# One 4 MB DMA for an expert's down weights, with gate and up columns read in runs of four

## The reference

```
z   = RMSNorm(x) @ W_in
a   = GatedDeltaNet(4 heads x 128)          chunks of 64
b   = DilatedSWA(8 heads x 64)              three (window, dilation) branches
h   = x + concat(a, b) @ W_out
out = h + MoE(RMSNorm(h))                   top 4 of 32 experts
```

```python
logits = hf @ w_router + b_router
top_v, top_e = lax.top_k(logits, 4);  gates = softmax(top_v)
# for every expert e and the tokens xblk that chose it:
gu   = xblk @ w_gu[e] + b_gu[e]                  # (tokens, 2048)
gate = minimum(gu[:, :1024], 7);  up = clip(gu[:, 1024:], -7, 7)
act  = (up + 1) * gate * sigmoid(1.702 * gate)
y    = act @ w_dn[e] + b_dn[e]                   # (tokens, 1024)
out += gate_weight * y
```

## Time and profile before

| | us |
|---|---|
| median of 3 runs | 1098.6 (1098.51 to 1100.0) |
| the profiled execution's own time | 1100.03 |
| its span | 1098.3 |
| PE busy | 1029.1 (94%) |
| DVE, ACT, POOL busy | 281.4, 162.4, 14.0 |
| bytes moved | 427.73 MB, 389 GB/s over the span |

### The profile page before, as it was taken

The page is one execution under the profiler, slowest core; times in us unless marked ns, Lnnn a source line. Parts: engine busy times, 40 slices in busy tenths (PEclk is TensorE's granted clock), DMA queues, the critical chain, the costliest instruction groups (busy, mean ns, idle before and its releaser), DMA issues.

```text
span 1098.3 us, 12632 instructions
## 1 busy us (share of the span) xinstructions
PE 1029.1 (94%) x4986; PEld 428.1 (39%) x4986; DVE 281.4 (26%) x667; ACT 162.4 (15%) x271; POOL 14.0 (1%) x34
## 2 busy tenths in 40 slices
PE   9999999999999999999999988888999898899987
PEld 7855566443434344443333222222333332233232
DVE  3754553522222232222211101111111111111111
ACT  4513355001000000001001000000000000000001
POOL 3001000000000000000000000000000000000000
PEclk9999998999999999999999989999999999999999
DMA  9577288799999999999999999999999999999996
GB/s 327 114 240 311 77 302 330 306 428 426 428 419 428 428 430 434 428 431 428 429 428 427 431 431 430 436 428 427 431 431 432 428 430 431 429 430 428 428 428 269
DMA packets 40186, 427.73 MB, mean 389 GB/s; under 512 B 8371, under 2 KB 10644, under 8 KB 20180
## 3 DMA queue, kind: packets, MB, share of 16 engines
q1 hardware_dynamic: 38884, 426.63, 93.3%
q10 hardware_dynamic: 1264, 0.56, 0.2%
HBM read 424.42 MB, written 2.75 MB: 389 GB/s over the span
## 4 chain that ended last, share of the span: by engine, by line
PE 52%; DMA 38%; DVE 6%; ACT 2%; issue 1%; SPq 0%; DVEq 0%; ACTq 0%
DMA store<-in_w_gate_up_dram 21%; PE bank L2036 18%; DMA store<-in_w_down_dram 16%; PE bank L2086 14%; PE bank L1590 3%; PE bank L1597 3%; PE bank L1953 2%; PE bank L1685 2%; PE bank L1817 2%; PE bank L2016 1%; DVE flow L1445 1%; PE bank L2055 1%; DVE flow L1438 1%; DVE flow L1443 1%; ACT flow L893 1%
## 5 line engine op out<-in xcount | busy, mean ns | idle before, releaser
L2036 PE MATMUL bank<-store,flow 128*64 128x512 f32 x2048 | 451.1, 596 | 14.1 <-DMA store<-in_w_gate_up_dram 13.2
L2036 PEld LDWEIGHTS bank<-store,flow 128*64 128x64 f32 x2048 | 144.2, 137 | 315.7 <-issue 288.8
L2086 PE MATMUL bank<-store,flow 128*64 128x512 f32 x992 | 227.6, 610 | 37.3 <-DMA store<-in_w_down_dram 25.0
L1438 DVE TENSOR_SCALAR flow<-bank 128x512 f32<-128x512 f32 x32 | 22.1, 691 | 605.5 <-PE bank L2036 605.5
L2086 PEld LDWEIGHTS bank<-store,flow 128*64 128x64 f32 x992 | 72.9, 140 | 171.0 <-issue 141.4
L893 ACT ACTIVATE flow<-flow 128x512 f32<-128x512 f32 x32 | 20.2, 630 | 448.4 <-DVE flow L1438 448.4
L1962 PE MATMUL bank<-qkT 64*128 64x512 f32 x248 | 61.9, 616 | 0.0
L1590 PE MATMUL bank<-store 128*128 128x512 f32 x128 | 57.2, 595 | 0.0
L909 ACT COPY qkT<-bank 128x512 f32<-128x512 f32 x31 | 18.1, 585 | 206.2 <-PE bank L2086 206.2
L903 ACT COPY flow<-flow 128x512 f32 x30 | 33.8, 1125 | 22.8 <-DVE flow L1419 13.3
L1962 PEld LDWEIGHTS bank<-qkT 64*128 64x128 f32 x248 | 21.3, 186 | 40.1 <-issue 40.1
(11 more groups left out here) (333 smaller groups left out, 598.1 us busy)
## 6 DMA issues: line engine op xcount, KB each, us to landing
store<-in_w_gate_up_dram SPq DMA_DIRECT2D x38, 4096.0 KB, 27.1
store<-in_w_down_dram SPq DMA_DIRECT2D x60, 2048.0 KB, 19.1
store<-in_w_gate_up_dram SPq DMA_DIRECT2D x51, 2048.0 KB, 15.2
store<-in_w_in_dram SPq DMA_DIRECT2D x6, 2048.0 KB, 15.9
store<-in_w_out_dram SPq DMA_DIRECT2D x1, 4096.0 KB, 12.9
store<-in_w_down_dram SPq DMA_DIRECT2D x3, 1024.0 KB, 30.7
store<-in_w_gate_up_dram SPq DMA_DIRECT2D x2, 1024.0 KB, 6.3
flow<-in_w_down_dram SPq DMA_DIRECT2D x1, 2048.0 KB, 11.8
```

Source lines behind the costliest of these rows:

```text
L1438: dve.tensor_scalar(gt, bank[4][:], LIMIT, None, ALU.min).then_inc(g_min, 1)
L2036: ins = mm(dst[SLOTS * hf:SLOTS * (hf + 1), :], rows[:, c:c + SLOTS], store[:, slot_at(j, odd) + c0:slot_at(j, odd) + c0 + 512], start=Fal ...
L2086: ins = mm(dst[SLOTS * hf:SLOTS * (hf + 1), :], turned[:, c:c + SLOTS], w[:, hf * 512:(hf + 1) * 512], start=f == 0, stop=f == KT - 1)
```

## The change

1. The down weights of a block are loaded in one DMA of 4 MB where `load_block` is called with `whole` (blocks 9 on), and for the first of the last three blocks with gate and up tiles apart (`whole_down=True`). Partition p holds rows 8p to 8p + 7 of the matrix, 32 KB in a run. The DMA waits until both down halves of the block before are used. TensorE's first down half then waits for the whole tile (`ld_tile[4]`), the second for nothing.
2. Half tiles that stay (early blocks, the last two) hold the rows 8p + 4h + c: 16 KB in a run, at a step of 32 KB in DRAM. The second half still waits for `ld_tile[5]`.
3. The activations have to come in that order. Half hf of the gate (and up) columns is now the columns 8r + 4hf + c, so the moving operand of L2036 reads four values and skips four.
4. The bias rows are put in the same order: the four bias DMAs bring 1024 (or 1020) columns each to `extra[:, 0:D]`, and one ACT copy takes four of every eight values into `bgu`. SP waits for this copy ahead of the load into `extra[:, 0:D]`, TensorE ahead of block 0.

```diff
+        bgu_rows = extra[:, 0:D]
...
-            half = tile - 4
-            src = w_down[0][e_ap, half * 4 * P:(half + 1) * 4 * P, :]
-            return src.rearrange("a (p c) n -> p (a c n)", p=P)
+            return w_down[0][e_ap, :, :].rearrange("a (p h c) n -> p h (a c n)", p=P, h=2)[:, tile - 4]
...
+        def expert_down(e_ap):
+            return w_down[0][e_ap, :, :].rearrange("a (p c) n -> p (a c n)", p=P)
+
+        def act_columns(ap):
+            return ap.rearrange("p (r h c) -> p h r c", h=2, c=4)
...
             for c in range(4):
-                sp.dma_start(bgu[N_EXP * c:N_EXP * (c + 1), :], b_gate_up[0][:, c * 512:(c + 1) * 512]
+                n = D - 4 * (c % 2)
+                sp.dma_start(bgu_rows[N_EXP * c:N_EXP * (c + 1), 0:n], b_gate_up[0][:, (c // 2 + 1) * D - n:(c // 2 + 1) * D]
                              ).then_inc(ld_moe, 16)
...
+            sp.wait_ge(bgu_ready, 1)
             sp.dma_start(extra[:, 0:D], expert_tile(slice(1, 2), 4)[:, 0:D]).then_inc(ld_extra, 16)
...
-            def load_down(m, e, off):
+            def load_down(m, e, off, whole):
+                if whole:
+                    sp.wait_ge(wdn_used, 2 * m + 2 * off)
+                    sp.dma_start(store[:, slot_at(8):slot_at(8) + 4 * SLOT], expert_down(bass.ds(e, 1))
+                                 ).then_inc(ld_tile[4], 16)
+                    return
                 for hf in range(2):
                     sp.wait_ge(wdn_used, 2 * m + (2 * off + hf - 1))
...
-            load_block(five_less, expert_of(five_less + 1), expert_of(three_less), 0, False, off=1, tiled=FINE_BLOCKS)
+            load_block(five_less, expert_of(five_less + 1), expert_of(three_less), 0, False, off=1, tiled=FINE_BLOCKS, whole_down=True)
...
+            act.wait_ge(ld_moe, 16 * 6)
+            Tally(act, bgu_ready).mark(act.copy(bgu.rearrange("p (r c) -> p r c", c=4),
+                                                bgu_rows.rearrange("p (r c) -> p r c", c=8)[:, :, 0:4]))
             h_sums(1)
...
                 if early and not b:
-                    pe.wait_ge(ld_moe, 16 * 6)
+                    pe.wait_ge(bgu_ready, 1)
...
-                order = [(bank[4], 0, 0), (bank[4], 1, 512), (bank[5], 0, 1024), (bank[5], 1, 1536)]
+                order = [(bank[4], 0, 0), (bank[4], 1, 0), (bank[5], 0, D), (bank[5], 1, D)]
...
-                                     store[:, slot_at(j, odd) + c0:slot_at(j, odd) + c0 + 512], start=False,
+                                     act_columns(store[:, slot_at(j, odd) + c0:slot_at(j, odd) + c0 + D])[:, hf], start=False,
...
-                elif not last:
-                    pe.wait_ge(ld_tile[4 + half], 16 * (b + 1) if early else 16 * b)
+                elif not last and half == 0:
+                    pe.wait_ge(ld_tile[4], 16 * (b + 1) if early else 16 * b)
+                elif not last and halves is not None:
+                    pe.wait_ge(ld_tile[5], 16 * halves)
```

More of the change, by code:

```diff
@@ L359, in hybrid_layer @@
         up_step, out_left, out_right, st_right = (sem(n) for n in ("up_step", "out_left", "out_right", "st_right"))
+        bgu_ready = sem("bgu_ready")
         seeded, cnt_read = sem("seeded"), sem("cnt_read")
@@ L546, in load_early, with load_block @@
                 sp.dma_start(tile_dst(4), expert_tile(slice(3, 4), 4)).then_inc(ld_tile[4], 16)
-            def load_block(m, e, e_next, down_at, whole, off=0, tiled=None):
+            def load_block(m, e, e_next, down_at, whole, off=0, tiled=None, whole_down=None):
                 odd = sp.value_load(parity[0:1, bass.ds(m + (off + 1), 1)], min_val=0, max_val=1)
@@ L554, in load_block @@
                     if half == down_at:
-                        load_down(m, e, off)
+                        load_down(m, e, off, whole if whole_down is None else whole_down)
                     if whole:
@@ L2065, in turns, with down @@
                 pe.wait_ge(SGT_ready, b + 1)
-            def down(b, half, last_at=None):
+            def down(b, half, last_at=None, halves=None):
                 last = last_at is not None
@@ L2088, in down, with rest @@
                 ins.then_inc(wdn_used, 1)
-            def rest(b, chunk=None):
+            def rest(b, chunk=None, halves=None):
                 turns(b, chunk)
@@ L2097, in rest @@
                     chunk_half(chunk, 1)
-                down(b, 1)
+                down(b, 1, halves=halves)
                 if chunk is not None:
@@ L2112, in first_rest @@
                 down(0, 0)
-                down(0, 1)
+                down(0, 1, halves=1)
                 pe.wait_ge(xs_ready, 2)
@@ L2129, in second_block @@
                 chunk_half(1, 0)
-                down(1, 1)
+                down(1, 1, halves=2)
                 pe.wait_ge(xs_ready, 3)
@@ L2137, in expert_block, with later_block @@
                 combine()
-                rest(b, chunk)
-            def later_block(b, odd, tiled=None):
+                rest(b, chunk, halves=None if isinstance(b, int) and b == FINE_BLOCKS - 1 else b)
+            def later_block(b, odd, tiled=None, halves=None):
                 gate_up(b, odd, whole=tiled is None, tiled=tiled)
@@ L2143, in later_block @@
                 combine()
-                rest(b)
+                rest(b, halves=halves)
             def table_block(b, odd):
@@ L2169, in last_two @@
                 turn_act(b + 1)
-                down(b, 1)
+                down(b, 1, halves=FINE_BLOCKS)
                 pe.wait_ge(actT_ready, b + 2)
@@ L2206, in _ @@
                 later_block(four_less, 0)
-                later_block(three_less, 1, tiled=FINE_BLOCKS + 1)
+                later_block(three_less, 1, tiled=FINE_BLOCKS + 1, halves=FINE_BLOCKS - 1)
                 last_two(two_less, 0)
             with pe.Else():
-                later_block(three_less, 0, tiled=FINE_BLOCKS + 1)
+                later_block(three_less, 0, tiled=FINE_BLOCKS + 1, halves=FINE_BLOCKS - 1)
                 last_two(two_less, 1)
```

## The result

The changed kernel takes 1102.56 us (median of 22 runs, 1099.77 to 1107.54); the kernel before, beside it, 1099.65 (22 runs, 1097.85 to 1102.53). The ratio is 1.0026, 95% interval 1.0017 to 1.0035: slower by 2.9 us, or 0.26%, where the forecast was 1.2 us slower and "no change that can be measured" the likeliest case. Part of the distance between 1099.8 and 1102.56 is not the change: the median of before was 1098.6 with three runs and is 1099.65 with 22. On the old base the ratio gives 1101.5, so 1.05 of the 2.8 us come from the base and 1.7 us from losses that were sized too small or left out.

A forecast was written before the change was run, and what follows sets the result against it. The DMA queue, never resting from about 200 to 1078 us, was taken as the bound. Rate -1.5, block 24 +1.8 and block 20 +0.9 gave +1.2 us: median 1098.6 to 1099.8, range 1096.6 to 1102.0.

The forecast's parts named there:

- What bounds the kernel: From about 200 to 1078 us the DMA queue never rests and sets the end; TensorE has about 4 us slack.
- Part 1: In 20 blocks, down weights in 32 KB runs raise the DMA rate, saving 1.5 us, range 1.5 to 2.8.
- Part 2: At blocks 20 and 24, later issue of down weights lets the DMA queue run dry: 0.9 and 1.8 us lost.
- Rival B: The DMA queue never runs out, since the 16 engines are spread in time; gain alone, 1097.1 us; chance 0.25.
- Part 3: Other waiting blocks, the tail, the bias copy on ACT and the larger bias DMAs: all put at nothing.
- SP's first issue still at 198.6: Sign of being right: SP's first issue for block 1 stays at 198.6 us, as it waits for TensorE.
- Part 4: Gate and up matmuls read four values, skip four: cost taken as nothing, upper bound 1.9 times.
- D: Strided read slows the gate and up matmuls, at 1.9 times about 1380 us; chance 0.05.
- F: The 32 KB run is cut in two on its way: no gain, only the droughts, 1101.3 us; chance 0.05.
- C: Low clock at both switches, blocks 20 and 24, through the down group (14.2 us): 1101 to 1104.5 us; chance 0.10.
- E: The DMA rate gains more, 0.14 us a block, with no drought: 1095.8 us; chance 0.10.
- A: The forecast itself: gain 1.5 to 2.8, two short droughts losing 0.5 to 6; 1097.0 to 1102.5 us; chance 0.45.

The follow-up runs named there:

- e9: The changed kernel unedited, run again on one chip beside two other versions; 1102.32 us, ratio 1.0019 to the kernel before.
- e5: Changed kernel with block 20's down weights alone issued in two halves, TensorE still waiting for the whole tile; 1102.01 us, ratio 1.0021.
- e6: Changed kernel with block 24's down weights alone issued in two halves, TensorE still waiting for the whole tile; 1100.76 us, ratio 1.0007.
- e1: Changed kernel's layout, but all down weights in two 2 MB DMAs, issued and waited for by halves as before; 1100.51 us, ratio 1.0008.
- e10: Same kernel as e1 (changed layout, all down tiles in halves with the old waits), run again; 1099.34 us, ratio 0.9998.
- e7: Changed kernel, but blocks 18 to 25 load down weights in halves with both engines' old waits; 1099.13 us, ratio 0.9996.
- e3: Changed kernel with down tiles of blocks 20 and 24 issued in halves, TensorE still waiting for all 4 MB; 1099.46 us, ratio 1.0012.
- e4: Changed kernel plus eight dummy matmuls ahead of the down tile wait in blocks 14 to 19 and 23; 1102.71 us, ratio 1.0031.
- e2: Changed kernel with the same late waits, but two 2 MB DMAs in place of the one of 4 MB; 1104.91 us, ratio 1.0045.
- mixed kernel: Changed kernel with down weights in halves and old waits in blocks 18 to 25; run as e7 and e11, ratios 0.9996 and 0.9988.
- e11: Same kernel as e7 (changed kernel, halves with old waits in blocks 18 to 25), run again; 1099.11 us, ratio 0.9988.
- e8: Changed kernel plus four dummy matmuls ahead of the down tile wait in blocks 14 to 19 and 23; 1101.01 us, ratio 1.0014.

## Why the prediction was right or wrong, by its steps

**What bounds the kernel: right.** Every kernel's time follows the DMA stream; no run shows TensorE's idle times mattering other than through SP's issues.

**Part 1, the gain of long runs, 1.5 us: right.** Groups at 931.06 and 960.19 are 29.13 us apart, the forecast period. Undisturbed, the two halves of a down tile land 4.89 and 4.90 us after what is ahead of them in the kernel before, 9.79 us in all, and the whole tile takes 9.71; over 20 tiles that is 1.5 us.

**Part 2, the mechanism: right.** Both droughts, at both places, with TensorE's idle times alternating between 2.5 and 4.0 us and every second group at 8.7 to 8.8 us, the clock at 0.50 behind the long ones. Block 23 was cold as taken, but not by the idle time that was read: the forecast had 7.8 us, measured are 4.16 and 4.15. It took the end of the turns from the old timeline, 856.06, but with the down groups waiting longer in every block the turns come later too (857.02, in a trace whose landings are 2.5 us ahead); for block 20 it had reckoned with this and got 4.1. Block 19, the one I couldn't tell, was warm in the first trace (+0.50 where the bound for warm was 0.6) and cold in the second (+1.88), e9:

```profile
754.00 8.78 PE L2106 MATMUL bank<-store,flow 128*64 128x512 f32 x32 [4.15 <-DMA store<-in_w_down_dram]
```

**What failed: two terms of the sum, the size of the droughts in Part 2 and the price that comes after them, which was put at nothing.** The first: the prediction took "the middle" of 0 and 3.7, 1.8 us for block 24; measured +2.11 and +2.58. For block 20 0.9; measured +0.50 and +1.88. The sum of 2.7 stands against 2.6 and 4.5, so on the droughts' own ground it was right in sum in the first trace, by luck (block 24 too low, block 20 too high), and low by 1.8 us in the second. The halving rested on the start of a DMA hiding under the one ahead. It hides only as far as SP issues ahead of that landing, 2.5 us for all of it (the table at e5 and e6), and with the low clock SP came only 0.7 to 0 us ahead.

When the last engine has run dry too, nothing is hidden: in e9 SP issues at 872.24, 0.47 us behind the last packet, and 4.19 MB land 11.8 us later where 9.7 are bytes. In the first trace the issue at 870.09 comes 0.2 us before the last engine is done, and the first new packets only start at 871.1. The Trainium skill (DMA: Bandwidth & Descriptors, Anatomy of one DMA) puts the fixed cost of a DMA, about 2 us for those that GpSimd issues, mostly at its completion. Here SP issues. The traces come near that size with 2.5 us, but not in that place: what a dry queue costs lies at the start, 1.0 us between issue and first packet, and 0.2 to 1.0 us more for each of these first packets than the 1.2 us of later ones.

The second term, missing altogether, is the price that comes later. Rival B named the distance between the engines as a cover for the start; it is none, but the drought takes the engines' leads away, and the fetches behind it then cost. In the landings after 900 us this was 1.56 and 1.47 us, less the 0.46 of before. With 1.1 for it, the forecast of +1.2 becomes +2.3, the first trace's value; that this fits so closely is luck too, since the sum for the droughts and the early fetches could each have moved it.

**Part 3: right**, as far as e1 and e10 can tell (ratios 1.0008 and 0.9998). The source view of the bias copy:

```profile
L898 ACT COPY store<-flow x1: 617/617/617, 177.3 to 177.3; 128x512 f32<-128x512 f32 x1
```

0.62 us, in idle time, between the forecast's 0.585 and 1.127. Only "SP's first issue still at 198.6" did not hold (196.41), and it was a bad sign to name: e1 and e10 are one kernel and have 196.65 and 198.86. Two of the three late executions (before, e7) have the granted clock at 0.5 from about 187 to 194 us; e10 at 198.86 has it full there, as that at 196.41 has, so the low clock is not the whole cause and it stays open.

**Part 4, the strided read, at nothing: right.** The page's costliest group after, 598 ns where the forecast wanted 592 to 596 and the kernel before has 596; e1, e3, e4, e6 and e7 have the same strided read and 596:

```profile
L2054 PE MATMUL bank<-store,flow 128*64 128x512 f32 x2048 | 452.0, 598 | 11.1 <-DMA store<-in_w_gate_up_dram 10.1
```

**Rivals.** B (no drought) falls with the dips, D with L2054, F with the period. C named both low clocks and a limit of 1101 to 1104.5; the first trace had one of them, e9 both. Of the six traces in which block 19 waits for a whole tile without dummies (the two of the change, e2, e3, e5, e6), five have it cold. Two cold switches, C's condition, are thus the common case and not one in ten: an error in the chances. C's size didn't come: a cold group took 8.6 to 9.8 us and not 14.2, and no drought cost more than 2.6. E falls too, the gain being the forecast one. The bounds given for A, 1097.0 to 1102.5, don't follow from its own terms either: 1098.6 less 2.8 plus 0.5 is 1096.3, less 1.5 plus 6 is 1103.1.

## What to carry to other kernels

Before joining two loads of a single-buffered tile, count what the queue still holds when the later wait ends, at the places where the order of issues changes and not in the mean; there keep the halves. Price a dry queue at issue-to-landing less the bytes, 2.5 us here, less the time by which the issue comes ahead of the last landing, not at half of it, and take that time with the clock that the engine behind the wait will have. Add what the levelled engines pay later. To compare two such kernels, measure a stretch between two fixed points of the stream. Here it agreed to 0.05 us over three traces without drought (before, e1, e10), where whole runs scatter over 5; but two traces of the mixed kernel differ by 0.5 and two of the changed one by 1.6, so one trace of each isn't enough.

## What the runs showed of the hardware that I had not expected

- One 16 KB instruction packet delays the DMA engine that it hits by about 1.55 us, and the landing by this less the lead of that engine over the last one. Over the fetch near 982 us the landing was 1.56, 1.27, 1.06 and 0.99 us late where the lead was 0, 0.27, 0.23 and 0.44 us (changed, e2, e5, e9), 0.20 and 0.11 late at 1.35 and 1.43 (e10, e7), and on time at 1.67, 1.81, 2.10, 2.17, 2.22, 2.30 and 2.66 (e4, e6, before, e11, e1, e3, e8). The distance from the first to the last engine doesn't tell this: it was 3.4 and 4.5 us in e10 and e7, which lost a little, and 1.8 in e4, which lost nothing.
- The distance of 4 us between engines with the same share of bytes looks like waste and is none by itself: each landing waits for the last engine, but the others' packets are done early and the queue loses nothing until it runs dry. In the kernel before it grows from 1.0 to 4.1 us in steps, each at a fetch that delays a landing (such as 0.8 us at 353, 0.5 at 479 and 0.9 at 614). These delays are a cost, 4.1 us from the first landing to 1079 us; the distance is what they leave behind.
- The code's size moves the fetches: the experiments with more loops have two to five more between 700 and 960 us (e3 at 765, 791, 873 and 900), where the others have none. In e3 that may be a part of the 0.0012 that is left; it was not separated. The mixed kernel has four more of them in each of its traces, and yet its delays outside of droughts add up to 4.2 and 4.3 us, hardly more than the 4.1 of before.
